# S5 stage: a recurrence for each tile with turn tables and scans, and across products of two tiles in turn

## What is computed

```python
h = rmsnorm(x, pre_gain)
u = h @ w_in                                  # 64 groups of 16 channels
# per group g, 64 complex states, decay a = exp(lam * dt), z = (a - 1) / lam
bu = einsum(z * b, u)                         # input of the states, each token
x_t = a * x_(t-1) + bu_t                      # recurrence over the 512 tokens
y = real(einsum(c, x)) + d * u
y = gelu(y)
y = y * sigmoid(y @ w_glu)
return y @ w_out
```

## Time and profile before

| | |
|---|---|
| runs | 1953.88, 1955.91, 1956.22 us |
| profiled execution | 1957.74 us, span 1956.0 us |
| TensorE busy | 1823.7 us (93%) |
| VectorE busy | 1050.7 us (54%) |
| ScalarE busy | 642.1 us (33%) |
| GpSimd busy | 58.8 us (3%) |
| fox stage | about 556 to 910 us |
| S5 input, recurrence, GLU | 1328.5 to 1529.5 us |

### The profile page before, as it was taken

The page is one execution under the profiler, slowest core; times in us unless marked ns, Lnnn a source line. Parts: engine busy times, 40 slices in busy tenths (PEclk is TensorE's granted clock), DMA queues, the critical chain, the costliest instruction groups (busy, mean ns, idle before and its releaser), DMA issues.

```text
span 1956.0 us, 21089 instructions
## 1 busy us (share of the span) xinstructions
PE 1823.7 (93%) x8489; PEld 1501.8 (77%) x8489; DVE 1050.7 (54%) x1598; ACT 642.1 (33%) x1008; POOL 58.8 (3%) x93
## 2 busy tenths in 40 slices
PE   2739999999899999999899999998799989999998
PEld 2728888888787777778788888887788878888887
DVE  5977766686635565556433336663841653434223
ACT  3344433322434343544322222233202442222222
POOL 5001300000000000000000000000011000000000
PEclk7659999999899888889999999999766999999999
DMA  9432333334331111111322223438733222333332
GB/s 370 164 159 86 97 98 97 101 109 136 114 111 56 42 44 44 43 33 44 119 97 97 97 97 121 137 115 216 208 92 102 83 97 97 97 97 97 97 97 76
DMA packets 125472, 209.47 MB, mean 107 GB/s; under 512 B 29520, under 2 KB 91328, under 8 KB 122176
## 3 DMA queue, kind: packets, MB, share of 16 engines
q1 hardware_dynamic: 125376, 208.13, 33.7%
HBM read 191.85 MB, written 16.24 MB: 106 GB/s over the span
## 4 chain that ended last, share of the span: by engine, by line
PE 79%; DVE 9%; DMA 4%; ACT 3%; SPq 2%; issue 2%; POOL 1%; DVEq 0%; ACTq 0%; PEldq 0%; POOLq 0%
PE bank L1661 24%; PE bank L1662 23%; PE bank L1663 23%; PE bank L2049 3%; DVE ada L1116 1%; DMA u_scratch<-us 1%; PE bank L1894 1%; SPq L606 1%; DMA rcnt<-in_rcnt 1%; PE bank L1701 1%; ACT prob L878 1%; PE bank L1890 1%; DVE w_lo L1031 1%; DMA raw<-in_dn 1%; DVE rinv L1299 1%
## 5 line engine op out<-in xcount | busy, mean ns | idle before, releaser
L1661 PE MATMUL bank<-hh,w_hi 128*128 128x512 f32 x1376 | 554.6, 403 | 8.1 <-POOL hl L1656 2.8
L1662 PE MATMUL bank<-hl,w_hi 128*128 128x512 f32 x1376 | 544.9, 396 | 0.0
L1663 PE MATMUL bank<-hh,w_lo 128*128 128x512 f32 x1376 | 542.7, 394 | 0.0
L1031 DVE TENSOR_TENSOR w_lo<-raw,w_hi 128x1024 fp32r<-128x1024 f32 x264 | 317.6, 1221 | 258.3 <-ACT w_hi L694 255.4
L694 ACT ACTIVATE w_hi<-raw 128x1024 fp32r<-128x1024 f32 x264 | 278.6, 1057 | 374.9 <-PE bank L1663 122.5
L1661 PEld LDWEIGHTS bank<-hh,w_hi 128*128 128x128 f32 x1376 | 265.1, 193 | 69.3 <-issue 8.4
L1662 PEld LDWEIGHTS bank<-hl,w_hi 128*128 128x128 f32 x1376 | 264.7, 192 | 57.7 <-issue 3.6
L1663 PEld LDWEIGHTS bank<-hh,w_lo 128*128 128x128 f32 x1376 | 264.1, 192 | 56.6
L1661 PE MATMUL bank<-w_hi,hid 128*128 128x512 f32 x528 | 206.9, 392 | 0.0
L1663 PE MATMUL bank<-w_hi,hid 128*128 128x512 f32 x528 | 205.6, 389 | 0.0
L1662 PE MATMUL bank<-w_lo,hid 128*128 128x512 f32 x528 | 205.5, 389 | 0.0
(11 more groups left out here) (262 smaller groups left out, 2133.0 us busy)
## 6 DMA issues: line engine op xcount, KB each, us to landing
raw<-in_up SPq DMA_DIRECT2D x132, 512.0 KB, 3.3
raw<-in_dn SPq DMA_DIRECT2D x60, 512.0 KB, 4.1
ada<-in_ada_w SPq DMA_DIRECT2D x24, 1024.0 KB, 9.6
raw<-in_fox_in SPq DMA_DIRECT2D x32, 512.0 KB, 3.3
raw<-in_s_w SPq DMA_DIRECT2D x24, 512.0 KB, 4.3
q_scratch<-q_tab SPq DMA_DIRECT2D x8, 576.0 KB, 4.4
q<-q_scratch SPq DMA_DIRECT2D x8, 576.0 KB, 5.1
w_scratch<-w_new SPq DMA_DIRECT2D x8, 512.0 KB, 5.1
```

Source lines behind the costliest of these rows:

```text
L1031: dve.tensor_tensor(w_lo[:, n % RING, :], raw[:, n % RING, :], w_hi[:, n % RING, :].bitcast(F32), ALU.subtract).then_inc(lo_done, 1)
L1661: pe.matmul(dst, w_h, r_h, start=first, stop=False, skip_group_check=True)
L1662: pe.matmul(dst, w_h, r_l, start=False, stop=False, skip_group_check=True)
L1663: return pe.matmul(dst, w_l, r_h, start=False, stop=last, skip_group_check=True)
```

## The change

- VectorE's recurrence is for one tile (16 instructions, 8 of them scans) and reads the state banks itself. It turns each state by the inverse of its phase (tables cos, sin in `turn`), so that a real decay `mag8` is left, scans the 64 blocks, and turns back. `recurrence(i - 2)` stands behind the split of slot i's successor weights, from input slot 2 on. The sem `rotated` frees the bank.
- GpSimd makes the tables: `unit_turn` (24 operations before the powers) and 16 times `turn_tables` (40 operations on 1 to 32 columns of two rows), each stored by SP in every second slot of the fox stage, and loaded as 256 KB a tile (`turn_load`).
- `across_two(i)` does tiles i and i + 1 together: 32 products that go alternately to the lower and upper rows, and so to the two tiles' banks; two waits on its own last product for a pair in place of four.
- `w3` is stored in its final layout (8 DMAs a tile in the down stages in place of 1) and loaded with 1; `w3` and `q2` have four buffers; `q2` is loaded without its first 16 columns.
- The orders on TensorE, ScalarE and SP are rewritten; inside and across use banks 0 to 3 for both halves, the GLU sums of slot m go to bank (m + 4) % 8.

```diff
-BANK_B = [0, 0, 4, 4, 4, 4]
+BANK_B = [0, 0, 4, 4, 0, 0]
...
-                        sp.dma_start(k_dram[i], kt[0:CH, :, :]).then_inc(k_out, 16)
+                        rows_of = w3_dram[i].rearrange("(c s) g m -> s c g m", s=BLK)
+                        for s in range(BLK):
+                            at_s = KPAD - CH * s
+                            sp.dma_start(rows_of[s], kt[0:CH, :, at_s:at_s + P]).then_inc(k_out, 16)
...
+            def turn_store(n):
+                if n % 2 == 0:
+                    k = n // 2
+                    sp.wait_ge(turn_new_done, k + 1)
+                    sp.dma_start(turn_dram[k // 2][:, :, 2 * (k % 2):2 * (k % 2) + 2, :], turn_new[:, :, :, :])\
+                      .then_inc(turn_out, 16)
+
             for j in range(KT):
                 for t, part in enumerate((0, 1, 3)):
                     load_fm(S_QKG + 3 * j + t, dram["fox_in"][4 * j + part])
+                    turn_store(3 * j + t)
             for idx in range(KT):
                 load_pairs(S_FO, idx, dram["fox_out"])
+                turn_store(3 * KT + idx)
...
+            def turn_load(i):
+                if i >= 2:
+                    sp.wait_ge(rec_done, i - 1)
+                sp.dma_start(turn[:, i % 2, :, :].rearrange("p t c -> p (t c)"),
+                             turn_dram[i].rearrange("p t r j -> p (t r j)")).then_inc(turn_in[i % 2], 16)
+
             def w3_load(i):
-                if i >= 2:
-                    sp.wait_ge(w3_mm, i - 1)
-                for s in range(BLK):
-                    sp.dma_start(w3[s::BLK, i % 2, :, :], k_dram[i][:, :, KPAD - CH * s:KPAD - CH * s + P])\
-                      .then_inc(w3_in[i % 2], 16)
+                if i >= TABS:
+                    sp.wait_ge(w3_mm, i - TABS + 1)
+                sp.dma_start(w3[:, i % TABS, :, :], w3_dram[i]).then_inc(w3_in[i % TABS], 16)
 
...
             for i in range(KT):
                 load_fm(S_S5I + RING + i, dram["s5_w"][RING + i])
                 u_write(i)
-                if 2 <= i < 6:
+                if i % 2 == 0:
+                    w3_load(i // 2)
+                else:
+                    q2_load(i // 2)
+                u_read(i)
+                if i >= 2:
                     w1_load(i)
-                    w3_load(i)
-                u_read(i)
-                if i == 2:
-                    load_gains(4)
+                    turn_load(i)
                 if i == 5:
-                    w1_load(6)
-                if i in (3, 4, 6):
-                    q2_load((3, 4, 6).index(i))
-            w1_load(7)
+                    y_write(0)
+                    y_write(1)
+                    y_read(0)
+                    y_read(1)
+            w3_load(4)
+            w3_load(5)
+            q2_load(4)
+            y_write(2)
+            y_write(3)
+            y_read(2)
+            y_read(3)
             w3_load(6)
             w3_load(7)
-            for i in range(KT):
+            for i in range(5, KT):
+                q2_load(i)
+            load_gains(4)
+            for i in (4, 6):
                 y_write(i)
-                if i + Q2S < KT:
-                    q2_load(i + Q2S)
+                y_write(i + 1)
                 y_read(i)
+                y_read(i + 1)
...
             def s5():
-                for i in range(KT):
+                for i in range(6):
                     hi(S_S5I + i + LEAD)
                     evict_u(i)
-                    if i >= 2:
-                        evict_states(i - 2)
-                evict_states(KT - 2)
+                gelu(0)
+                gelu(1)
+                hi(S_GLU + 1)
+                evict_u(6)
+                hi(S_GLU + 2)
+                evict_u(7)
+                high_y(0)
+                high_y(1)
                 hi(S_GLU + 3)
-                evict_states(KT - 1)
+                gelu(2)
+                gelu(3)
                 hi(S_GLU + 4)
-                half_out(0)
-                half_out(4)
+                high_y(2)
+                high_y(3)
+                for i in range(4, KT):
+                    gelu(i)
+                for i in range(4, KT):
+                    high_y(i)
...
+            def recurrence(i):
+                p, x = i % 2, xs[:, i % 4, :, :, :].rearrange("p t r j -> p t (r j)")
+                b = bank[6 + p][:, :].rearrange("p (t c) -> p t c", t=2)
+                shape = [P, 2, 4 * NBLK]
+                cos = turn[:, p, 0, :].unsqueeze(1).to_broadcast(shape)
+                sin = turn[:, p, 1, :].unsqueeze(1).to_broadcast(shape)
+                same, cross = t_same[:, :, :], t_cross[:, :, :]
+                dve.wait_ge(st_mm, i + 1)
+                dve.wait_ge(turn_in[p], 16 * (i // 2 + 1))
+                own.add(dve.tensor_tensor(same, b, cos, ALU.mult))
+                own.add(dve.tensor_tensor(cross, b[:, ::-1, :], sin, ALU.mult))
+                own.settle()
+                dve.sem_inc(rotated, 1)
+                own.add(dve.tensor_tensor(same[:, 0, :], same[:, 0, :], cross[:, 0, :], ALU.add))
+                own.add(dve.tensor_tensor(same[:, 1, :], same[:, 1, :], cross[:, 1, :], ALU.subtract))
+                own.settle()
                 for t in range(2):
...
+                    for r in range(4):
+                        cols = slice(NBLK * r, NBLK * r + NBLK)
+                        decay = mag8[:, 4 * i + r:4 * i + r + 1].to_broadcast([P, NBLK])
+                        own.add(dve.tensor_tensor_scan(cross[:, t, cols], decay, same[:, t, cols], 0.0, ALU.mult, ALU.add))
+                own.settle()
+                if i >= 4:
+                    dve.wait_ge(out_mm, i - 3)
+                own.add(dve.tensor_tensor(same, cross, cos, ALU.mult))
+                own.add(dve.tensor_tensor(x, cross[:, ::-1, :], sin, ALU.mult))
+                own.settle()
+                own.add(dve.tensor_tensor(x[:, 0, :], same[:, 0, :], x[:, 0, :], ALU.subtract))
+                own.add(dve.tensor_tensor(x[:, 1, :], same[:, 1, :], x[:, 1, :], ALU.add))
+                own.settle()
                 dve.sem_inc(rec_done, 1)
...
             def s5():
-                for i in range(6):
+                for i in range(KT):
                     lo(S_S5I + i + LEAD)
-                recurrence(0)
+                    if i >= 2:
+                        recurrence(i - 2)
                 lo(S_GLU + 3)
-                recurrence(1)
+                recurrence(KT - 2)
                 lo(S_GLU + 4)
+                recurrence(KT - 1)
...
+            def turn_tables(k):
+                pairs = slice(2 * k, 2 * k + 2)
+                re, im = turn_new[:, 0, :, :], turn_new[:, 1, :, :]
+                if k:
+                    pool.wait_ge(turn_out, 16 * k)
...
+                for e in range(6):
+                    n = 2 ** e
+                    last = min(2 * n + 1, NBLK)
+                    src, dst, w = slice(1, last - n), slice(n + 1, last), last - n - 1
+                    m_re = re[:, :, n:n + 1].to_broadcast([P, 2, w])
+                    m_im = im[:, :, n:n + 1].to_broadcast([P, 2, w])
+                    t1, t2 = turn_t[:, 0, :, 0:w], turn_t[:, 1, :, 0:w]
+                    own.add(pool.tensor_tensor(t1, re[:, :, src], m_re, ALU.mult))
+                    tt(t2, im[:, :, src], m_im, ALU.mult)
+                    tt(re[:, :, dst], t1, t2, ALU.subtract)
+                    own.add(pool.tensor_tensor(t1, re[:, :, src], m_im, ALU.mult))
+                    tt(t2, im[:, :, src], m_re, ALU.mult)
+                    tt(im[:, :, dst], t1, t2, ALU.add)
+                pool.sem_inc(turn_new_done, 1)
...
+            for k in range(PAIRS // 2):
+                turn_tables(k)
...
-            def across(i):
-                p = i % Q2S
-                pe.wait_ge(rec_done, i // 4 + 1)
-                pe.wait_ge(q2_in[p], 16 * (i // Q2S + 1))
-                for h in range(2):
-                    for g in range(h, 8, 2):
+            def across_one(i, g, t):
+                return pe.matmul(bank[i % 4][:, NBLK * g + 1:NBLK * g + NBLK], q2[rows(g), i % TABS, t, g // 2, :],
+                                 xs[rows(g), i % 4, t, g // 2, 0:NBLK - 1],
+                                 start=False, stop=g >= 6 and t == 1, skip_group_check=True)
+
+            def across_two(i):
+                for j in (i, i + 1):
+                    pe.wait_ge(q2_in[j % TABS], 16 * (j // TABS + 1))
+                pe.wait_ge(rec_done, i + 2)
+                for swap in range(2):
+                    for r4 in range(4):
                         for t in range(2):
-                            mm = pe.matmul(bank[i][:, NBLK * g + 1:NBLK * g + NBLK], q2[rows(g), p, t, g // 2, CH:QW],
-                                           xs[rows(g), i // 4, t, 4 * (i % 4) + g // 2, 0:NBLK - 1],
-                                           start=False, stop=g == 7 and t == 1, skip_group_check=True)
+                            across_one(i + swap, 2 * r4, t)
```

(37 more changed lines are left out.)

162 lines of the change are left out of this document (70 added, 92 removed).

## The result

The changed kernel takes 1960.9 us (median of 6 runs, 1959.9 to 1964.1) against 1956.1 for the kernel before: ratio 1.0028, 95% interval 1.0015 to 1.0041. It is slower by about 5 us, where 26 us less had been forecast. The profiled execution has a span of 1959.0 us against 1956.0.

A forecast was written before the change was run, and what follows sets the result against it. S5's 201.0 us were taken to hold 52.8 lost, 15.9 idle and 37 of half clock. S5 -29 and fox +2.5 gave -26.5 us, so 1930 us; forecast band 1912 to 1938, 8-in-10 range 1910 to 1959.

The forecast's parts named there:

- Part 6: Down stages: eight w3 stores for one add 3.5 us of SP issue a tile, covered by kt waits; cost nothing.
- Parts 1 to 4: S5 stage: recurrence, TensorE order, across in pairs and queues together bring it from 201.0 to 172 us, 29 less.
- Part 5: Fox stage: GpSimd's tables cost 2.5 us, 1 of waits at the start and 1.5 of slowed VectorE operations.
- (a): S5 across pairs: row halves don't overlap, a pair takes 8.0 us and not 4.3; 1955.5 us in all; chance 0.22.
- (b): S5 slots 2 to 7: DMA landings stay at 6 to 8 us, +13 us, 1943 in all; chance 0.17.
- (c): Fox stage: SP waits for each table with raw weights queued behind; 87 us at 0.7 an operation, 2018; chance 0.13.
- (d): S5 recurrence: a VectorE tile costs 9 us, not 6.3, cutting the gain to 5 to 10; about 1949; chance 0.08.
- The slow side: Whole kernel: slower than before, made up of (c) and a sixth of (a); chance 0.17.

The follow-up runs named there:

- e1: The changed kernel with the eight w3 stores of a tile (but a down stage's last) moved on SP behind the next raw weight load; 1933.9 us, ratio 0.9872.
- b1: The kernel before, with only its single kt store a tile moved behind the next raw weight load; 1957.2 us, ratio 0.9992.
- e3: The changed kernel with GpSimd making only the first turn table, which SP stores 16 times; 1958.9 us, ratio 1.0001.
- e5: The changed kernel with a pair's across products in the old order, tile by tile and one row half at a time; 1982.0 us, ratio 1.0131.
- e4: The changed kernel with turn tables made and stored in every second slot of the second up stage, not in fox; 1996.9 us, ratio 1.0193.

## Why the prediction was wrong

**Part 6, "free or nearly", is the step that failed.** It priced seven added stores a tile at nothing, since SP waits 33.0 us for `kt` alone. The measured cost was 12.3 and 13.0 us, 25 together. Without it the changed kernel would have been 22 us faster than before by the two profiles, and it was 25 faster in e1; with it it was 3 slower by the profiles and 5 by the medians. The 3.5 us of issue were sized nearly right (4.25 us for eight, 3.9 more than for one). What was wrong was taking a wait for slack. The wait of SP for kt was the last piece of a loop that already took as long as TensorE's own work (b1: no gain from shortening it), and the raw load stood behind it on the same queue. The text even named what a failed cover would cost, 3 us a tile at a load of raw weights, and that is what it cost: 25.3 us over eight tiles, 3.2 each. But the cover that it named was the wait itself. The row that would have told is ScalarE's 15.28 us idle for raw weights, in the same stage.

**Parts 1 to 4, the S5 stage: right.** Forecast 29 us less; measured 29.6 less. The split came as forecast too: 11.1 us more idle and 40 less busy (17.2 by the pairs, 23 by the clock), measured 11.3 and 40.9. How the 40.9 divide between pairs and clock no run shows by itself. A recurrence tile 6.3 forecast, 5.9 measured. A pair 4.3, measured 4.07 + 0.31. The wait at inside(3) 9, measured 13.5; at across_two(2) 5, measured 4.9; at the GLU parts 3 and 8, measured 1.0 and 6.1: 25.5 in sum, against 27 with the 2 for late weights. The path over SP from the end of the first pair to inside(3) was short by 5.5, 22.5 us and not 17: SP issued the store of y 4.2 us after the pair's end, since it was still at the loads w1 and turn, where 0.6 had been reckoned, and from there to the first read it took 4.8 us, not 2.6.

**Part 5, fox: sign and order of size right, mechanism not shown.** 2.5 forecast, 1.5 of it for longer VectorE operations and 1 for waits for tables; 5.5 in the one pair of profiles, 3.3 as the mean over 13. SP did wait for tables at the start of the stage, 25.0 us in four waits (longest 9.3) where 0 to 8 had been forecast, but no wait of TensorE in fox was for weights, so the tables did not pace the stage. A table's operations took 10 to 16 us against 18 forecast; GpSimd's 600 there ran at 0.24 us each. The lock that the Trainium skill, "SBUF — State Buffer", section "Who interferes with whom", describes did not show here as longer VectorE operations, as the earlier trace rows had shown it for large ones; it showed on GpSimd's side (1.18 us against 0.20, under e3).

**The rivals.** (a), no overlap of row halves: refuted by e5, where its price (8.0 a pair at the full clock) shows only in the old order. (b), congested transfers: no, median landings in the S5 input slots were 3.0 to 6.4 us by kind (1.9 for the small y reads) and the stage still took the time forecast. (c), tables that pace SP: not in fox, where SP's 25.0 us of waits for them reached nobody, but real, as e4 shows, with 38 us. (d): no, a recurrence tile took 5.9 us. The slow side was reached by a mechanism that was not among them, and the chance of 0.17 given to it hung on another cause. With the raw loads first, the change is worth 25 us (e1, 0.9872), near the forecast.

## What to carry to other kernels

An engine's or a queue's wait is slack only if what stands behind it is not awaited by the one it waits for; follow the wait once round before an instruction is taken to cost nothing there. Where eight small DMAs are needed, put the large load that others wait for ahead of them, and ahead of the wait in front of them: the same stores cost 25 us in front of that load and nothing behind it. When work is paced by slots, work out its period against the slots of the very stage it is put into: 14.7 us a table fitted two slots of fox (25 us), and not two of the up stage (10.9).

## What was not expected of the hardware

Products on alternate row halves (and alternate banks), with weights of 128 columns, took half the time each, as if two ran at a time (64 records in 4.07 us), and TensorE's granted clock stayed at 1.00 through them; the same products in one half at a time, behind the same work, took 10.96 us, and the clock had fallen to a mean of 0.72. Eight scans of 64 columns took 0.20 us each, a sixth of what the 512-column one took (1.22). An eighth would be 0.15, so the fixed cost of one is some 0.05 us (estimate from these two).
